# Third layer's attention: transposed maps in six banks, value products of two heads in alternation, second query unit behind the scores

## What is computed

```python
bias = jnp.where(col_ok[None, None], rpb_bias, -jnp.inf)
s_lat = jnp.einsum('bqhd,bkwhd->bhqkw', qr, kb) * scale + bias
s_ctx = jnp.einsum('bqhd,bnhd->bhqn', qr, kz) * scale
p = jax.nn.softmax(jnp.concatenate([s_lat, s_ctx], -1), axis=-1)
out_x = (p_lat @ vb + p_ctx @ vz) @ w_o
# context tokens: plain attention over the context alone
out_z = softmax(qz @ kz.T * scale) @ vz @ w_o
```

## Time and profile before

| | us |
|---|---|
| median of 3 runs | 2513.4 |
| lowest, highest | 2512.65, 2514.22 |
| the profiled execution | 2513.73 |
| its span in the trace | 2512.0 |
| third layer's attention on PE, query unit 0 to last value product | 1524.9 to 1711.0 |

### The profile page before, as it was taken

How to read it: one execution, slowest core, us unless ns; L and a number is a source line. 1 busy time by engine, 2 the same in 40 slices (tenths; PEclk the granted TensorE clock), 3 DMA queues, 4 the chain that set the end, 5 groups by cost and what they waited for, 6 DMA issues and landing times.

```text
span 2512.0 us, 37089 instructions
## 1 busy us (share of the span) xinstructions
PE 2440.7 (97%) x12228; PEld 1990.1 (79%) x12228; DVE 1272.1 (51%) x2283; ACT 967.7 (39%) x1944; POOL 1095.8 (44%) x839
## 2 busy tenths in 40 slices
PE   8999799999999999999999999999999999998998
PEld 4566688888877777888888887778888888777998
DVE  6889876647233322236665243555765524475211
ACT  3455343332233332333323243554422324465653
POOL 0322344445434334334445443223444543434996
PEclk9999899999999999999999999999999999999999
DMA  8362345546222222235555323222555532322553
GB/s 325 118 116 78 144 172 200 196 163 226 87 94 76 70 72 91 77 101 201 195 193 186 104 83 93 76 84 93 187 187 190 192 117 81 100 84 84 185 184 133
DMA packets 117186, 341.65 MB, mean 136 GB/s; under 512 B 35568, under 2 KB 36848, under 8 KB 116336
## 3 DMA queue, kind: packets, MB, share of 16 engines
q1 hardware_dynamic: 109072, 335.01, 39.2%
q10 hardware_dynamic: 8032, 5.52, 1.4%
HBM read 335.80 MB, written 4.69 MB: 136 GB/s over the span
## 4 chain that ended last, share of the span: by engine, by line
issue 50%; PE 23%; POOL 21%; DVE 2%; ACT 1%; DMA 1%; POOLq 1%; SPq 0%; DVEq 0%; ACTq 0%
POOL w_lo L557 21%; PE low_banks L564 17%; PE high_banks L564 6%; DMA gain_f<-in_final_g 1%; PE low_banks L751 0%; DVE tmp L1747 0%; POOLq L556 0%; ACT w_hi L1160 0%; DVE dump L1676 0%; POOLq L551 0%; ACT lnm L1184 0%; DVE h_lo L1755 0%; ACT ssum_rstd L1185 0%; DVE tmp L1975 0%; DMA ada_raw<-in_ada_w 0%
## 5 line engine op out<-in xcount | busy, mean ns | idle before, releaser
L557 POOL TENSOR_TENSOR w_lo<-w_raw,w_hi 128x512 fp32r<-128x512 f32 x832 | 1095.3, 1344 | 1397.6 <-ACT w_hi L1160 1396.9
L564 PE MATMUL low_banks<-h_hi,w_hi 128*128 128x512 f32 (+1 forms) x1792 | 643.6, 359 | 14.8 <-POOL w_lo L557 7.7
L1160 ACT ACTIVATE w_hi<-w_raw 128x512 fp32r<-128x512 f32 x832 | 473.9, 624 | 420.9 <-PE low_banks L564 199.6
L564 PE MATMUL low_banks<-h_lo,w_hi 128*128 128x512 f32 (+1 forms) x1792 | 634.6, 354 | 0.0
L564 PE MATMUL low_banks<-h_hi,w_lo 128*128 128x512 f32 (+1 forms) x1792 | 634.4, 354 | 0.0
L564 PEld LDWEIGHTS low_banks<-h_hi,w_hi 128*128 128x128 f32 x1792 | 340.7, 190 | 70.8 <-issue 11.2
L1603 DVE SCALAR_TENSOR_TENSOR ssum_rstd<-ada_raw,high_banks 128x1024 f32<-128x1024 f32 x304 | 370.7, 1220 | 40.8 <-DMA ada_raw<-in_ada_w 32.5
L564 PEld LDWEIGHTS low_banks<-h_lo,w_hi 128*128 128x128 f32 x1792 | 340.7, 190 | 47.9 <-issue 1.9
L564 PEld LDWEIGHTS low_banks<-h_hi,w_lo 128*128 128x128 f32 x1792 | 340.7, 190 | 46.2
L1511 ACT ACTIVATE lnm<-low_banks 128x512 f32<-128x512 f32 (+1 forms) x88 | 47.9, 544 | 430.2 <-PE low_banks L564 430.1
L2175 DVE TENSOR_TENSOR tmp<-low_banks,lnm 128x512 f32<-128x512 f32 (+1 forms) x88 | 55.0, 625 | 290.0 <-ACT lnm L1511 286.3
(11 more groups left out here) (216 smaller groups left out, 3669.7 us busy)
## 6 DMA issues: line engine op xcount, KB each, us to landing
w_raw<-in_weights SPq DMA_DIRECT2D x424, 512.0 KB, 3.6
ada_raw<-in_ada_w SPq DMA_DIRECT2D x152, 512.0 KB, 3.8
ada_first<-in_ada_w SPq DMA_DIRECT2D x28, 512.0 KB, 7.8
ada_rest<-in_ada_w SPq DMA_DIRECT2D x12, 512.0 KB, 7.2
bias<-rpb_skew SPq DMA_DIRECT2D x64, 64.0 KB, 2.4
rpb_skew<-rpb_rows ACTq DMA_DIRECT2D x1, 3556.0 KB, 32.8
cond_l<-in_cond SPq DMA_DIRECT2D x3, 1024.0 KB, 4.4
xT<-in_xT SPq DMA_DIRECT2D x2, 1024.0 KB, 9.0
```

Of the source, the lines that this page charges most:

```text
L557: nc.gpsimd.tensor_tensor(out=w_lo[:, r, part], in0=w_raw[:, r, part], in1=w_hi[:, r, part], op=ALU.subtract).then_inc(lo_ready, 1)
L564: return nc.tensor.matmul(dst, lhsT, rhs, start=start, stop=stop, **kw)
L1160: nc.scalar.activation(w_hi[:, r, part], w_raw[:, r, part], ACT.Copy).then_inc(hi_ready, 1)
```

## The change

Three edits. (1) `turned_bank`: head 1's groups go to banks 4, 5 and 1 in place of 1, 2 and 0, and the groups alternate between the heads; only the last group (head 1, group 0, bank 1) waits for a copy, the first one. ACT copies in the same alternating order. (2) `weighted` goes over the four products and issues head 0's and head 1's next to each other; it waits for 2, 4 and 6 copies in place of 1, 2, ... 6. (3) Query unit 1 is no longer run ahead of the scores of tile 0; tile 1 runs its own, behind them. Layers 1 and 4 (one map for a tile) get the same instructions in the same order as before.

```diff
--- before.py
+++ after.py
@@ -214,6 +214,11 @@
     return ((7, 6) if L.zq else (6, 7))[m] if m < 2 else OUT_REST[m - 2]
 
 
+def turned_bank(g, sub):
+
+    return (1, 4, 5)[g] if sub else g
+
+
 def da_banks(L):
 
     return (3, 7) if L.zq else (LAST_O, LAST_MS)
@@ -735,51 +740,46 @@
 
                 order = [g for g in range(1, per)] + [0]
 
-                def transposes(t, sub):
-
-
-                    for p, g in enumerate(order):
-                        if sub == 1:
-
-                            pe.wait_ge(L.aT_ready, t * L.groups + (p + 1))
-                        for c in range(4):
-                            kb, qb = (c // 2, c % 2) if g == 0 else (g + 1, c) if L.zq else (2 + c // 2, c % 2)
-                            src = n_x[:, qb % 2, sub, :] if L.na else a_x[:, qb % 2, :]
-                            if qb >= 2:
-                                src = n_z[:, sub, qb - 2, :] if L.na else a_z[:, qb - 2, :]
-                                kb -= 2
-                            last = nc.tensor.transpose(bank[g][:, c * P:c * P + P], src[:, kb * P:kb * P + P],
-                                                       ident[:, :])
-                        last.then_inc(L.t_done, 1)
-
-                def values_product(t, sub, dst):
-
-                    lo, hi = (64 * sub, 64 * sub + 64) if L.na else (0, P)
+                def transposes(t, g, sub):
+
+                    if sub and g == 0:
+
+                        pe.wait_ge(L.aT_ready, t * L.groups + 1)
+                    for c in range(4):
+                        kb, qb = (c // 2, c % 2) if g == 0 else (g + 1, c) if L.zq else (2 + c // 2, c % 2)
+                        src = n_x[:, qb % 2, sub, :] if L.na else a_x[:, qb % 2, :]
+                        if qb >= 2:
+                            src = n_z[:, sub, qb - 2, :] if L.na else a_z[:, qb - 2, :]
+                            kb -= 2
+                        last = nc.tensor.transpose(bank[turned_bank(g, sub)][:, c * P:c * P + P], src[:, kb * P:kb * P + P],
+                                                   ident[:, :])
+                    last.then_inc(L.t_done, 1)
+
+                def turn(t):
+
+                    pe.wait_ge(L.a_ready, t + 1)
+                    for g in order:
+                        for sub in range(subs):
+                            transposes(t, g, sub)
+
+                def weighted(t, dst):
+
+                    pe.wait_ge(L.vst_ready, t + 1)
                     copies = 0
                     for j, kb in enumerate((2, 3, 0, 1)):
                         if kb >= 2 and L.zq:
                             g, a, w = kb - 1, 0, TOK
                         else:
                             g, a, w = kb // 2, (kb % 2) * SEQ, SEQ
-                        if order.index(g) == copies:
-                            copies += 1
-
-                            pe.wait_ge(L.aT_ready, t * L.groups + (per * sub + copies))
-                        mov = (nT[:, sub, g, a:a + w] if L.na else aT[:, g, a:a + w])
-                        last = mm(bank[dst][lo:hi, 0:w], v_st[:, kb, lo:hi], mov, j == 0, j == 3)
-                    return last
-
-                def turn(t):
-
-                    pe.wait_ge(L.a_ready, t + 1)
-                    for sub in range(subs):
-                        transposes(t, sub)
-
-                def weighted(t, dst):
-
-                    pe.wait_ge(L.vst_ready, t + 1)
-                    for sub in range(subs):
-                        last = values_product(t, sub, dst)
+                        fresh = order.index(g) == copies
+                        copies += fresh
+                        if fresh:
+
+                            pe.wait_ge(L.aT_ready, t * L.groups + subs * copies)
+                        for sub in range(subs):
+                            lo, hi = (64 * sub, 64 * sub + 64) if L.na else (0, P)
+                            mov = (nT[:, sub, g, a:a + w] if L.na else aT[:, g, a:a + w])
+                            last = mm(bank[dst][lo:hi, 0:w], v_st[:, kb, lo:hi], mov, j == 0, j == 3)
                     last.then_inc(L.pv_done, 1)
 
                 def mean_square(t, dst):
@@ -807,8 +807,7 @@
                     if place >= 2:
 
                         pe.wait_ge(L.y_lo_ready, t - 1)
-                    if place != 1:
-                        unit(t * 2 + n, slot, bank[6], H, L.W).then_inc(unit_used, 1)
+                    unit(t * 2 + n, slot, bank[6], H, L.W).then_inc(unit_used, 1)
                     if place == 0:
                         copied()
                     unit(t * 2 + (n + 1), slot + 1, bank[7], H, TOK).then_inc(unit_used, 1)
@@ -817,11 +816,6 @@
                         pe.wait_ge(L.qk_act, t + 1)
                         turn(t - 1)
                         weighted(t - 1, 6)
-
-                    if place == 0:
-
-                        pe.wait_ge(L.qk_act, 1)
-                        unit(n + 2, slot + 2, bank[6], H, L.W).then_inc(unit_used, 1)
 
                     pe.wait_ge(L.qk_dve, t + 1)
                     pe.wait_ge(L.qk_act, t + 1)
@@ -1324,14 +1318,14 @@
 
                 def turned(t):
 
-                    per = L.groups // (2 if L.na else 1)
-                    order = [g for g in range(1, per)] + [0]
+                    subs = 2 if L.na else 1
+                    order = [g for g in range(1, L.groups // subs)] + [0]
                     for p in range(L.groups):
-                        g = order[p % per]
+                        g, sub = order[p // subs], p % subs
 
                         act.wait_ge(L.t_done, t * L.groups + (p + 1))
-                        dst = nT[:, p // per, g, :] if L.na else aT[:, g, :]
-                        nc.scalar.activation(dst, bank[g][:, :], ACT.Copy).then_inc(L.aT_ready, 1)
+                        dst = nT[:, sub, g, :] if L.na else aT[:, g, :]
+                        nc.scalar.activation(dst, bank[turned_bank(g, sub)][:, :], ACT.Copy).then_inc(L.aT_ready, 1)
 
                 def ahead(c, i=0):
 
```

## The result

The changed kernel takes 2496.05 us (median of 6 runs, 2494.96 to 2497.12), beside 2513.64 for the kernel before (6 runs); the ratio is 0.9929, 95% interval 0.9917 to 0.9942. The forecast was 2496.8 in a range of 2493.3 to 2500.3. The profiled execution has a span of 2493.2 us, 18.8 less than before.

A forecast was written before the change was run, and what follows sets the result against it. PE was taken to bound third-layer attention until DVE's chain takes over; gains 5.39 + 8.05 + 1.23 + 1.98 = 16.65 us off 2513.73 give 2497.1, less 0.3 to the median: 2496.8, range 2493.3 to 2500.3.

The forecast's parts named there:

- The product: Third layer's attention, each tile's value product: both heads' column halves run at once, 2.72 us against 4.50, gain 1.78.
- Transposes and copies: Each tile's 24 transposes on PE: 2.70 us where 2.85 were taken with three waits for copies, gain 0.15.
- The chain that is late next: DVE's mask meets POOL's third subtraction; `a_ready` at T+19.56 (T: transposes' start), tile 19.66, gain 1.61 not 1.93.
- (b): Five further tiles after the third tile's transposes start, each 1.61 us shorter: 8.05.
- (a): Up to the third tile's transposes: their start at 1570.04 instead of 1575.43, 5.39 us sooner.
- (c): Last interval between tiles, 20.39 us and already bound by the chain: the mask ends 1.23 sooner, gain 1.23.
- (d): Last transposes and product, in `project`: 0.20 + 1.78 = 1.98 us gained.
- 1.5 either way: Whole kernel: allowance of 1.5 us for where stretches at the low clock fall; nothing taken from later layers.
- The other side: Value products: alternation drains the array on top of no overlap, each of eight costs 0.66 more, 2522 us; chance 0.03.
- the first three outcomes: Forecast (0.63); mask slips between subtractions, 2494.5 (0.12); head 1 one instruction behind, product 3.2, 2498.5 (0.10).

The follow-up runs named there:

- e3: Changed kernel with six banks and alternating transposes kept, but products issued head 0 then head 1 as before: 2508.77 us, stage (qT's first copy to last product) 176.02.
- e8: Changed kernel with the mask left out, its place on DVE reading a score bank in PSUM, same size and place: 2494.33 us, stage 161.42.
- edit 2: Query unit 1 put behind the scores of tile 0 instead of ahead; alone on the kernel before: 2509.8 us.
- e1: Kernel before with only query unit 1 moved behind the scores of tile 0: 2509.8 us, ratio 0.9984, stage 176.91.
- e7: Kernel before with the mask's addition moved on DVE to right behind the copy of kT: 2512.52 us, ratio 0.9995, stage 178.38.
- e5: Changed kernel with the mask's addition moved on DVE to right behind the copy of kT, before y_lo: 2493.2 us, stage 161.09.

## Why the prediction was right, and where its terms were off

It was right in its mechanism and within 0.8 us in the whole. By its own steps:

- **The product.** Forecast 2.72 from 4.50, measured 2.73; e3 puts the old order back and loses 12.95 of the stage. The Trainium skill (TensorE: Matmul & The Clock Gate, Part 3) has weight loads overlap a running matmul only where the row groups differ. The trace does not agree: these two column halves share all rows, and in the third tile head 1's first weights were loaded from 1572.75 to 1572.89 while head 0's first matmul ran (1572.75 to 1573.39). That nothing at all would overlap by this rule was the prediction's own step; the rule speaks of weight loads.
- **Transposes and copies.** 2.70 forecast, 2.73 to 2.74 measured (2.71 where PE had not waited before them).
- **The chain that is late next.** The mask was to be issued at T+6.99, to end at T+9.07; it was issued at T+7.06 and ended at T+9.11. e8 shows the cause. `a_ready` was forecast at T+19.56 in each tile and came at 19.59 in the third, but at 19.22 to 19.36 in the others. **This is the term that was mis-sized:** (b), 5 x 1.61 = 8.05, measured 21.27 x 5 - 97.48 = 8.9. The 10.48 from the mask's end to the last normalising were read in one tile, the first of the loop. In the four others of the trace of before they are 10.13 and 10.26 in turn. The difference lies right behind the mask, before the first addition of the bias. It starts 0.50 after the mask's end in the third tile, 0.14 in the fourth and 0.27 in the fifth; here the fourth and the fifth in the kernel before:

```profile
1605.62 1.40 DVE L1988 TENSOR_TENSOR bias<-bias,na_mask 128x1024 f32<-128x1024 f32 x1
1607.15 0.43 DVE L1935 TENSOR_TENSOR low_banks<-low_banks,bias 128x256 f32<-128x256 f32 x1
...
1626.89 1.39 DVE L1988 TENSOR_TENSOR bias<-bias,na_mask 128x1024 f32<-128x1024 f32 x1
1628.55 0.43 DVE L1935 TENSOR_TENSOR low_banks<-low_banks,bias 128x256 f32<-128x256 f32 x1 [0.27 <-DVE bias L1988]
```

  One tile was taken for five. So of the tiles of 19.66 that were forecast one came near (19.73), and the others took 19.37 to 19.51.
- **(a), edit 2.** 5.39 forecast, 5.42 measured (1575.43 to 1570.01); scores at 1536.76 (1536.78 forecast). e1 separates it: 3.6 for edit 2, of which some 1.5 is the low clock (first transposes to the next scores took 8.86 in the kernel before and 7.38 in e7). e7 shows that this part was not certain: the same idle stretch was followed by the full clock there, and edit 2 would then be worth 2.1, an estimate.
- **(c), (d).** 1.23 and 1.98 forecast; 1.21 (20.39 to 19.18) and 1.89 (8.86 to 6.97 from the last transposes to the product's end).
- Together 16.65 forecast, 17.4 measured in the stage. The span fell by 18.8; the other 1.4 lie after the stage (800.9 to 799.6), where a stretch at the low clock behind the fourth layer's attention lasted 6.8 us in place of 10.2. The forecast had left this to its 1.5 either way. Whether it belongs to the change is not shown: the changed kernel's second profile has 6.8 there again, all eleven profiles of other kernels have 10.2, and the medians differ by 17.6 only, 0.2 more than the stage.
- The other side did not come: no drain at an alternation (the product took what the sum without one gave), and no wait for copies.
- The range was 3.5 about the forecast. The 1.5 about the first three outcomes, which it was said to take in, would be 2493.0 to 2500.0 in place of 2493.3 to 2500.3; nothing hangs on that.

## What to carry to other kernels

Where two products use 64 columns of the array each, and write different halves of a bank's partitions, issue them alternately: these float32 products ran at once (2.73 us for what took 4.50). When such a cut shortens the bounding engine's tile, shift everything that hangs on it by that much and look what it now meets: here an addition slid into POOL's subtractions and took 0.8 us longer. An operation with two inputs in SBUF that does not depend on the tile's data belongs where POOL is idle and nothing waits. It pays only where its chain binds: 1.97 us in e5, nothing in the middle tiles of e7.

## What was not expected of the hardware

- The same idle stretch of PE, 2.74 us at the same place of the program, was followed by transposes at a mean granted clock of 0.65 and 0.61 in two kernels' traces and of 1.00 in a third (e7).
- Between POOL's subtractions, issued without a gap, DVE's waiting addition always came first. In all seven tiles of the changed kernel that have it, the mask waited 0.8 us (1.0 in the second tile), never for a second subtraction, and the next subtraction took 2.27 to 2.29 in place of 1.27.
- The step from the mask to the first addition of the bias costs 0.50, 0.14 or 0.27 us by the tile of the loop, at the same tiles in the kernel before and in both profiles of the changed one; it makes the tiles 19.73 and 19.37 to 19.51. That the addition waits for the mask is not the whole of it: in e8 it waits for the row before it just the same, and starts 0.03 behind it in every tile. There DVE's wait for the first score bank stands ahead of that row and not behind it. What makes the step differ from tile to tile stays open.
